# Neighbourhood attention in pairs of tiles, with the softmax rows divided on GpSimd ahead of the turn

## What is computed

```python
logits = einsum('bhcd,bhicjd->bhcij', qr, kr) * scale + bias
p = softmax(logits.reshape(b, h, GRID_W, wr * NA_WIN_C), axis=-1)
out = einsum('bhcij,bhicjd->bhcd', p, vr)
...
y = concatenate([out_a * silu(g_a), out_b * silu(g_b)], axis=-1)
x = x + y @ w_out[l]
```

## Time and profile before

| | us |
|---|---|
| median of 3 runs | 941.54 (941.08 to 941.77) |
| the profiled execution | 941.23 |
| its span in the trace | 939.4 |
| PE busy with matmuls | 906.4 (96%) |
| DVE busy | 587.7 (63%) |
| ACT busy | 450.7 (48%) |
| POOL busy | 70.3 (7%) |

### The profile page before, as it was taken

One profiled execution on the slowest core, in us unless ns is written; L12 is line 12 of the kernel. 1 busy time (PEld: TensorE's weight loads), 2 busy tenths in 40 slices (PEclk: granted clock), 3 DMA queues, 4 the chain that ended last, 5 costly groups with the idle time before them and its releaser, 6 DMA issues.

```text
span 939.4 us, 14917 instructions
## 1 busy us (share of the span) xinstructions
PE 906.4 (96%) x5861; PEld 715.3 (76%) x5861; DVE 587.7 (63%) x1200; ACT 450.7 (48%) x962; POOL 70.3 (7%) x89
## 2 busy tenths in 40 slices
PE   3999999999999999999999999999999999999996
PEld 1689888865667788887888877888887788887785
DVE  5899798998886472438862448344255965335733
ACT  4734223666784243436925348233434863436631
POOL 1001130006300010000010000000000010000002
PEclk9999999999999999999999999999999999999999
DMA  9735636266000232332304224122243222333203
GB/s 380 312 109 125 181 136 180 102 209 239 1 2 23 90 129 90 112 101 76 111 8 150 90 90 134 43 90 90 90 155 92 62 91 89 94 100 118 72 0 90
DMA packets 34647, 104.71 MB, mean 111 GB/s; under 512 B 14929, under 2 KB 14929, under 8 KB 32146
## 3 DMA queue, kind: packets, MB, share of 16 engines
q1 hardware_dynamic: 28098, 85.77, 27.5%
q0 software_dynamic: 3824, 15.73, 5.2%
q10 hardware_dynamic: 2656, 2.26, 1.0%
HBM read 98.37 MB, written 4.19 MB: 109 GB/s over the span
## 4 chain that ended last, share of the span: by engine, by line
PE 88%; DVE 6%; ACT 2%; issue 2%; DMA 1%; SPq 0%; POOL 0%; POOLq 0%; DVEq 0%; ACTq 0%
PE bank L1023 81%; PE bank L1384 2%; PE bank L1522 2%; DMA ring<-in_w_ada 1%; PE bank L1364 1%; DVE ring L2083 1%; PE bank L1440 1%; DVE arena L1651 0%; DVE ring L2282 0%; ACT ring L834 0%; PE bank L1430 0%; ACT arena L715 0%; DVE soft L2115 0%; ACT w_hi L882 0%; DVE soft L2093 0%
## 5 line engine op out<-in xcount | busy, mean ns | idle before, releaser
L2138 DVE TENSOR_TENSOR w_lo<-ring,w_hi 128x1024 fp32r<-128x1024 f32 x80 | 97.8, 1225 | 114.6 <-ACT w_hi L882 111.5
L1023 PE MATMUL bank<-w_hi,hT_hi 128*128 128x512 f32 x320 | 125.3, 392 | 1.3 <-issue 1.0
L1023 PE MATMUL bank<-hT_hi,w_hi 128*128 128x512 f32 x320 | 126.3, 395 | 0.0
L1023 PE MATMUL bank<-hT_lo,w_hi 128*128 128x512 f32 x320 | 124.6, 389 | 0.0
L1023 PE MATMUL bank<-hT_hi,w_lo 128*128 128x512 f32 x320 | 124.6, 389 | 0.0
L1023 PE MATMUL bank<-w_lo,hT_hi 128*128 128x512 f32 x320 | 124.6, 389 | 0.0
L1023 PE MATMUL bank<-w_hi,hT_lo 128*128 128x512 f32 x320 | 124.5, 389 | 0.0
L882 ACT ACTIVATE w_hi<-ring 128x1024 fp32r<-128x1024 f32 x80 | 84.4, 1058 | 11.6 <-PE bank L1023 11.4
L1023 PEld LDWEIGHTS bank<-w_hi,hT_hi 128*128 128x128 f32 x320 | 60.1, 188 | 14.7 <-issue 2.6
L1023 PEld LDWEIGHTS bank<-hT_hi,w_hi 128*128 128x128 f32 x320 | 60.1, 188 | 14.0 <-issue 0.7
L1023 PEld LDWEIGHTS bank<-hT_lo,w_hi 128*128 128x128 f32 x320 | 60.1, 188 | 12.8
(11 more groups left out here) (323 smaller groups left out, 1814.1 us busy)
## 6 DMA issues: line engine op xcount, KB each, us to landing
ring<-in_w_units SPq DMA_DIRECT2D x80, 512.0 KB, 3.6
ring<-in_w_ada SPq DMA_DIRECT2D x4, 2048.0 KB, 10.2
bias_ring<-in_na_bias POOLq DMA_DIRECT2D x8, 1024.0 KB, 5.5
ring<-in_w_out SPq DMA_DIRECT2D x2, 2048.0 KB, 8.7
bias_ring<-in_t_bias POOLq DMA_DIRECT2D x8, 448.0 KB, 3.8
x_t<-in_x SPq DMA_DIRECT2D x4, 512.0 KB, 5.9
arena<-in_w_ada SPq DMA_DIRECT2D x1, 2048.0 KB, 20.3
arena<-in_w_ada SPq DMA_DIRECT2D x2, 1024.0 KB, 23.2
```

Of the source, the lines that this page charges most:

```text
L1023: return pe.matmul(out, lhsT, rhs, start=first, stop=last)
L2138: dve.tensor_tensor(w_lo[:, u % 4], raw_w[:, u % 4], w_hi[:, u % 4].bitcast(fp32), SUB).then_inc(S["w_split"], 1)
```

## The change

Four things change in the stage, and one small thing elsewhere.

1. `na_scale`, new, on POOL: for each tile, after the reciprocals are there, multiplies the two 128x256 halves of `prob2` by their `rinv`, in place. PE's turn now waits for `na_scaled` instead of `na_exp`. The two products against the identity and the first of `na_out`'s two multiplications are dropped. The bias loads of the second half of the pairs are issued by POOL behind every fourth tile's scaling.
2. PE's loop goes in steps of two: scores of tiles j and j + 1, turns of j - 3 and j - 2, weighings of j - 5 and j - 4.
3. The lag of moves on ACT and turns on PE behind the exponential is three tiles (`NA_LAG`) instead of two, and DVE's `na_out` comes two steps later.
4. The first half (four of eight steps) of the output product's rows 0 and 1 is done ahead: row 0's before the turn of tile 15, row 1's behind the last weighing. Then both second halves follow. Before, row 0 and row 1 were each done in one piece.
5. In the first block, PE's wait for `kc_used` is dropped ahead of its wait for `vblk_ready`; DVE waits for its own copy as before.

The diff, cut to its core (the semaphores' names, and the lines of DVE's loop whose step numbers shift by two, are left out):

```diff
+        NA_LAG = 3
...
+            def na_scale(l, m):
+
+                M = N_NA * l + m
+                pool.wait_ge(S["na_rinv"], M + 1)
+                for e in range(2):
+                    r = (2 * M + e) % 16
+                    p = prob2[:, m % 8, e * KW:(e + 1) * KW]
+                    pool.tensor_scalar(p, p, rinv[:, r:r + 1], None, MUL).then_inc(S["na_scaled"], 1)
...
-                for n in range(at_ + DAH + 2, min(at_ + LOADS + 2, LOADS * LAYERS)):
-                    load_bias(n)
+                for m in range(N_NA):
+                    na_scale(l, m)
+                    if m % NT == NT - 1 and at_ + DAH + 2 + m // NT < LOADS * LAYERS:
+                        load_bias(at_ + DAH + 2 + m // NT)
...
-                        na_move(l, 0)
-                        for j in range(N_EARLY, N_NA + 2):
-                            na_move(l, j - 2)
+                        for j in range(N_EARLY, N_NA + NA_LAG):
+                            na_move(l, j - NA_LAG)
...
-                    pe.wait_ge(S["na_exp"], 2 * M + e + 1)
+                    pe.wait_ge(S["na_scaled"], 2 * M + e + 1)
...
-                pe.wait_ge(S["na_rinv"], M + 1)
-                for e in range(2):
-                    hf = slice(e * HD, (e + 1) * HD)
-                    r = (2 * M + e) % 16
-                    ins = mm(out[hf, KW + m % 2 * P:KW + (m % 2 + 1) * P], rinv[:, r:r + 1].to_broadcast([P, HD]), ident, False, m % 2 == 1)
...
-                        for j in range(N_EARLY, N_NA + 3):
-                            if j < N_NA:
-                                na_score(l, j)
-                            if j == N_EARLY:
-                                pe.wait_ge(S["proj_evac"], pt2(l, 8) - 1)
-                                na_turn(l, 0)
-                                pe.wait_ge(S["proj_evac"], pt2(l, 8))
-                            if j < N_NA + 2:
-                                na_turn(l, j - 2)
-                            na_weigh(l, j - 3)
+                        na_score(l, N_EARLY)
+                        pe.wait_ge(S["proj_evac"], pt2(l, 8) - 1)
+                        na_turn(l, 0)
+                        for j in range(N_EARLY + 1, N_NA + 4, 2):
+                            for m in (j, j + 1):
+                                if m < N_NA:
+                                    na_score(l, m)
+                            for m in (j - NA_LAG, j + 1 - NA_LAG):
+                                if m == 1:
+                                    pe.wait_ge(S["proj_evac"], pt2(l, 8))
+                                if m < N_NA:
+                                    na_turn(l, m)
+                            for m in (j - NA_LAG - 2, j - NA_LAG - 1):
+                                if m >= 0:
+                                    na_weigh(l, m)
+                            if j == N_NA:
+                                out_rows(0, 6, range(0, 4))
+                        na_weigh(l, N_NA - 1)
+                        out_rows(1, 7, range(0, 4))
...
-                tt(y, o[:, 256:512], y, MUL)
                 dve.tensor_tensor(y, o[:, 0:256], y, MUL).then_inc(S["na_out"], 1)
```

More of the change, by code:

```diff
@@ L267, in build @@
             "v_done", "state_ready", "y_done", "y_evac", "y_out", "y_back", "x_back", "q_stats", "q_rstd", "q_ready",
-            "q_T", "q_evac", "y_pre", "y_tanh", "y_gelu", "glu_done", "glu_tanh", "ssm_ready", "cs_done", "cs_taken", "kc_used", "cs_ready",
+            "q_T", "q_evac", "y_pre", "y_tanh", "y_gelu", "glu_done", "glu_tanh", "ssm_ready", "cs_done", "cs_taken", "na_scaled", "cs_ready",
             "cs_exp", "cp_ready", "cp_T", "cp_evac", "gate_tanh",
@@ L1280, in _ @@
                     pe.transpose(bank[7][:, 0:64], kc_sb[0:64, 0:P], ident[0:64, 0:64]).then_inc(S["kc_T"], 1)
-                    pe.wait_ge(S["kc_used"], 1)
                     pe.wait_ge(S["vblk_ready"], 1)
@@ L1450, in tile_T, with tile_tok @@
                 return ins
-            def tile_tok(out, l, g, i, order=range(KD), between=None):
+            def tile_tok(out, l, g, i, order=range(KD), between=None, steps=range(KD)):
                 tok = slice(i * P, (i + 1) * P)
-                for m, k in enumerate(order):
+                for m in steps:
+                    k = order[m]
                     u = first_unit(l, g) + m // 2
@@ L1535, in na_weigh @@
                         hf = slice(e * HD, (e + 1) * HD)
-                        mm(out[hf, m % 2 * P:(m % 2 + 1) * P], src[:, b0 + b, (2 * p + e) * HD:(2 * p + e + 1) * HD],
-                           probT2[:, m % 4, e * KW + b * P:e * KW + (b + 1) * P], m % 2 == 0 and b == 0, False)
-                pe.wait_ge(S["na_rinv"], M + 1)
-                for e in range(2):
-                    hf = slice(e * HD, (e + 1) * HD)
-                    r = (2 * M + e) % 16
-                    ins = mm(out[hf, KW + m % 2 * P:KW + (m % 2 + 1) * P], rinv[:, r:r + 1].to_broadcast([P, HD]), ident, False, m % 2 == 1)
+                        ins = mm(out[hf, m % 2 * P:(m % 2 + 1) * P], src[:, b0 + b, (2 * p + e) * HD:(2 * p + e + 1) * HD],
+                                 probT2[:, m % 4, e * KW + b * P:e * KW + (b + 1) * P], m % 2 == 0 and b == 0, m % 2 == 1 and b == 1)
                 ins.then_inc(S["na_weighed"], 1)
@@ L1617, in _ @@
+                        na_weigh(l, N_NA - 1)
+                        out_rows(1, 7, range(0, 4))
                 pe.wait_ge(S["na_taken"], 2 * N_NA * (l + 1))
-                pe.wait_ge(S["mixT_lo"], 4 * (l + 1))
-                def na_ready():
-                    pe.wait_ge(S["na_lo"], N_NA // 2 * (l + 1))
-                for t in range(8):
+                pe.wait_ge(S["na_lo"], N_NA // 2 * (l + 1))
+                for t in range(2):
+                    out_rows(t, 6 + t, range(4, KD)).then_inc(S["wo_done"], 1)
@@ L1624, in _ @@
+                for t in range(2, 8):
                     c, i = divmod(t, 4)
-                    if t >= 2:
-                        pe.wait_ge(S["x_ready"], 8 * (l + 1) + t - 1)
+                    pe.wait_ge(S["x_ready"], 8 * (l + 1) + t - 1)
                     hook = None
-                    if t == 0:
-                        hook = na_ready
-                    elif t == 7 and l + 1 < LAYERS:
+                    if t == 7 and l + 1 < LAYERS:
                         hook = lambda: (rows_T(l + 1, 0), rows_T(l + 1, 1))
@@ L2004, in _ @@
             kc = kc_sb[0:64, 2 * HD:3 * HD]
-            dve.tensor_copy(kc, bank[5][0:64, 0:HD]).then_inc(S["kc_used"], 1)
-            dve.wait_ge(S["kc_used"], 1)
+            settle(dve.tensor_copy(kc, bank[5][0:64, 0:HD]))
             dve.tensor_tensor_reduce(kc_sb[0:64, 0:HD], kc, kc, 1.0, 0.0, MUL, ADD, ss[0:64, 48:49]).then_inc(S["k_stats"], 1)
@@ L2342, in _ @@
                                 na_inverse(l, j - 1)
-                            if j >= 5 and j % 2:
-                                na_out(l, (j - 5) // 2)
                             if j >= 7 and j % 2:
-                                na_lo(l, (j - 7) // 2)
-                            if j >= 5 and j % 2:
-                                na_hi(l, (j - 5) // 2)
+                                na_out(l, (j - 7) // 2)
+                            if j >= 9 and j % 2:
+                                na_lo(l, (j - 9) // 2)
+                            if j >= 7 and j % 2:
+                                na_hi(l, (j - 7) // 2)
                             if j - MIX_LAG in MIX_AT:
@@ L2352, in _ @@
                         na_inverse(l, N_NA - 1)
-                        for g in range(N_NA // 2 - 2, N_NA // 2):
+                        for g in range(N_NA // 2 - 3, N_NA // 2):
                             na_out(l, g)
```

6 lines of the change are left out of this document (4 added, 2 removed).

## The result

The changed kernel takes 948.78 us (median of 4 runs, 947.97 to 950.12) against 941.65 us for the kernel before in the same comparison: **a ratio of 1.0077, interval 1.0059 to 1.0094**. The prediction was 939.5 us with a range up to 944.0. Its profiled execution took 949.35 us with a span of 947.5 us, 8.1 us more than the 939.4 before.

What follows compares the result with a forecast made beforehand. The stage was taken as bound by PE's own issue, with ACT hardly less loaded and limiting the gain. Per layer -2.3 + 0.3 + 0.3 + 0.4 + 0.3 = -1.0 us, two layers -2.0: 939.5 us, range 937.2 to 944.0.

Steps and rivals of the forecast that it cites:

- term (2): POOL's two scalings per tile: 0.40 us each, 0.8 a tile against ACT's 1.47, so hidden in throughput.
- PE's saving: Dropped sums and grouped scores, turns and weighings shorten PE's queue by 6.5 us per layer, 13 us in all.
- ACT's ceiling: ACT's unchanged work in the stage leaves at most -2.3 us a layer; 936.9 us if all additions hide.
- The wait at score 5: PE waits some 2.0 us at score 5 until tile 3 is taken, adding 0.3 us a layer through ACT.
- The port: POOL's scalings stand still beside DVE ops reading two SBUF tensors: 0.3 us a layer, bounds 0 and 1.0.
- Bias loads late: Rival: the load for tiles 8 to 11 still takes 8.1 us, delaying exp 8; 943.5 us, chance 0.14.
- POOL slow: Rival: 0.75 us per scaling, 1.50 a tile, exceeds ACT's 1.47; about 2 us more a layer, 943.5 us, chance 0.13.
- The clock falls: Rival: PE's waits at score 5 and later lower its clock; one fall 941.2 us, two 942.9, chance 0.14.
- The signs named: Trace signs of a wrong forecast: scalings over 0.6, bias waits above 1.5 us, PEclk below 1, ACT gaps above 1 us.

Runs made afterwards that it cites:

- e14: Changed kernel with the first half row of the output product ahead of turns 13 and 14; 946.33 us, ratio 1.0053.
- e9: e2 with VectorE's take of tile 3 moved ahead of its last split of a weight; 936.46 us, ratio 0.9948 to the kernel before.
- e1: Changed kernel without POOL's scaling, rows left undivided, pairs kept; 938.21 us, ratio 0.9965.
- e2: Changed kernel without POOL's scaling, with the sums back on TensorE and VectorE's second product back (pairs only); 940.91 us, ratio 0.9993.
- e15: Changed kernel with the first half row earlier and the take of tile 3 ahead of the last weight split; 946.20 us, ratio 1.0049.
- e4: Changed kernel with both heads of a tile scaled by one two-input POOL instruction instead of two one-input ones; 944.88 us, ratio 1.0040.
- e8: Changed kernel with the second head of each tile scaled on VectorE, only the first on POOL; 943.72 us, ratio 1.0029.
- e5: e2 with the pairing begun one tile later; 940.18 us, ratio 0.9992 to the kernel before.
- e3: Changed kernel with POOL's scaling kept but TensorE's loop back to single tiles, output product not split; 949.03 us, ratio 1.0081.
- e7: Changed kernel with each scaling over 128 of its 256 columns; 941.84 us, ratio 1.0007.

## Why the prediction was wrong

**The step that failed is term (2), the scaling on POOL.** The prediction put it between 0.30 us (a cast's cost per column) and 0.75 (half of a two-input instruction of 512 columns, with a fixed part), took 0.40 "near the cast's lower side, since a scaling by one number per partition also reads one tensor", and called it "hidden in throughput". It measured 0.912 at the least and 0.964 in the mean. The upper bound was none: it supposed that one input can't cost more than two. A tile takes POOL 1.93 us instead of 0.80.

The prediction's own sum comes near the stage that was measured once that term is put right, and meets it once the place of the first half row is counted too. POOL starts on tile 3 at 566.08; 13 tiles of 1.93 us and three bias loads of 0.78, 0.74 and 0.61 give 593.3, and with its 1.1 us of waits, 594.4 (measured 594.46). With the half row done by then, turn 15 0.6, values 13 to 15 1.6, the second half row 2.8 and 24 products 5.4 end at 604.9. The half row wasn't done: turn 15 came at 596.99, and 596.99 + 10.4 = 607.4; the row's add started at 607.51. The order was the second thing that the sum hadn't seen, since with 0.40 the tile would have been scaled before TensorE got there; e14 shows it to be worth 2.3 us in all.

Point by point:

- *PE's saving*: right. The pair of scores takes 0.9 us, the pair of turns 1.03 (564.80 to 565.83 in e9), the sums are gone, and e9's 2.5 us in layer 1 is the 2.3 of grouping.
- *ACT's ceiling*: right, as a ceiling. Without the scaling the stages are 1.7 and 2.3 us shorter, against "-2.3 us a layer is the most", and 938.2 us. e1, whose scaling costs nothing, comes within 1.3 us of the forecast of 939.5.
- *The wait at score 5*: 1.90 us against 2.0. But the prediction priced it at 0.3 us a layer. In a stage bound by TensorE the wait, with the fall of the clock behind it, costs nearly all that the pairs save: e2 and e9 differ by its cause, 4.2 us by their ratios. In the changed kernel POOL covers it (e14 and e15 come out alike).
- *The port*: 0.3 us a layer was no good size but a good suspect. In the changed kernel a scaling takes 0.05 us more in the mean than at its shortest, so POOL loses at most 26 x 0.05 = 1.4 us a layer to it (an estimate). It decides e4 and has a part in e8.
- *Bias loads late*: not here. VectorE waited 0.3 us for one in layer 0's stage. They do hold e5 (1.9 and 1.6) and layer 0 of e9 (1.3), where all else is faster.
- *POOL slow*: the rival was the right mechanism with the wrong end: 0.75 us a scaling and 943.5 us, and a chance of 0.13. The slope it implies, 2 us a layer from 0.40 to 0.75, is too small for what follows once POOL passes 1.47 us a tile: each further 0.1 us a scaling is 13 x 0.2 = 2.6 us a layer.
- *The clock falls*: they came, though at more places than one: in layer 0 the granted clock was 0.66 over 562 to 572 us and 0.84 over 582 to 592. Two falls were put at 942.9, on top of a forecast that didn't hold. e3 loses as much without them, and e4's layer 0 is 1.8 us longer than before (52.35) at a granted clock of 1.00 throughout. What they cost in the changed kernel no run isolates; that it is part of its 8 us is argued only from e14's four runs.
- The signs named did show it: scalings over 0.6, a granted clock below 1 near 566, and ScalarE with gaps above 1 us (2.18 before 584.76).

## What to carry to other kernels

When work moves to an engine on which the trace has no row of that operation, work out first the duration at which that engine becomes the bound (here 1.47 / 2 = 0.74 us a scaling), and if the price's bounds come near it, let the range of the time follow the engine past it. A row of another kind, even one with more inputs, is no upper bound. And a regrouping that saves issue time paid here only once the first wait of the new order was gone: pairs alone gave 0.07%, which is no more than the noise, the earlier take alone nothing, both together 0.5%.

## What the runs showed that I had not expected

- A POOL scaling of 256 f32 columns costs 0.91 us, and one of 128 columns 0.60. A cast costs 0.61 for 512, and a two-input product with a repeated second input 1.04 for 512. The Trainium skill, "GPSIMD Engine Reference", section 4.1 "Engine selection", calls one-input work on this engine roughly line-rate; here the scaling takes 2.6 times VectorE's 0.354 (e8), and the measurement decides.
- VectorE and POOL hold each other up in both directions: a VectorE subtraction with two SBUF inputs went from 0.41 to as much as 1.98 us beside POOL's bias issue and two-input product (e4), and POOL's scaling from 0.91 to 1.60 beside such a subtraction, but only to 1.08 beside VectorE's scaling (e8).
- The 1.9 us wait at score 5 was followed by the lower clock in the changed kernel's layer 0 and not in e7's, whose granted clock was 1.00 over 562 to 592 us with the same wait. In e7's layer 1, with the same wait again, it was 0.83 over 862 to 872. The wait alone doesn't decide it.
